# Two expert tiles per store in the dense expert-dot stage of a two-block transformer kernel

## The chip, the cores and the metric

The kernel runs as one program on one core of a Trainium2 chip. The metric is the device time of the whole program in microseconds (us); lower is better. TensorE is called PE here, ScalarE ACT, VectorE DVE, GpSimd POOL and SyncE SP.

## The reference, cut to what matters

512 tokens of 1024 features go through two blocks. The first block ends in a PEER layer: each token chooses 8 x 16 of 16,384 experts, takes the dot of its vector with each chosen expert's row of `peer_u`, applies GELU, weighs it, and sums the chosen rows of `peer_v`.

```python
def chunk_fn(args):
    hx, ix, gx = args
    u = peer_u[ix]
    a = jax.nn.gelu(jnp.einsum('td,thkd->thk', hx, u), approximate=False)
    vsel = peer_v[ix]
    return jnp.einsum('thk,thkd->td', gx * a, vsel)
```

The second block (a convolution, attention and pooling mixer, then 16 experts with 2048 hidden features that each choose their tokens) follows it.

## The kernel before

Of the PEER layer, 128 tokens are computed sparsely (rows gathered by indirect DMAs from POOL) and the other 384 (`DENSE`) densely. The dense part has two stages that concern us.

**First stage** (`peer_first_phase`, class `ExpertDots`). The 16,384 experts are 128 tiles of 128. For a tile, SP loads 512 KB of `u_tiles` (`load`, L548); ACT writes the rounded high part of it (`split_scalar`, a cast recorded at L82); POOL writes the low part (`split_pool`, recorded at L87); PE makes 24 matmuls of 128x384 into one of two PSUM banks (`dot`, L566); ACT applies GELU from the bank into one of two halves of the SBUF buffer `gelu` (`activate`, L574) and then issues, on its own DMA queue, a store of 192 KB to the DRAM tensor `expert_dots` (L577). There are three slots for the loaded tile, one of which lies in `one_h_row` and `one_acts`. Two semaphores `stored[0]` and `stored[1]` tell when the store of each half has landed, and GELU of tile t waits for the store of tile t-2. PE's dots of tile t wait for GELU of tile t-2, which frees the bank.

The order on ACT is written out by hand: split of tile t+2, GELU and store of tile t, and so on. The first 54 tiles run in a loop of 6. From tile 56 on, other work is interleaved: 48 sets of 8 tokens, three for every four tiles, for which DVE builds one-hot matrices, ACT scales them (`gate_set`, L1278), PE makes 16 small matmuls (L1260), and ACT copies the product out (`stage_set`, L1287). After GELU of tile t, ACT does `stage_set` of the set that stood behind tile t-1 on PE and `gate_set` of the one that will stand behind tile t+1. No set stands behind a tile whose number leaves 3 when divided by 4. In this half SP also stores the weights that come of it (`expert_weights`, L1201), POOL gathers `peer_u` rows for the sparse tokens, and DVE reduces them (L1400).

At the end SP loads the first `peer_v` rows and stored dots of the second stage, stores the last weights (3 MB), waits for these, loads the first weights (L2270), and waits for the stores of the dots (L1221). The next stage begins after all engines have ended the first.

**Second stage** (`peer_value_phase`, class `ValueRows`): 64 turns of two expert tiles. Per turn SP reads 384 KB of stored dots (`load_dots`, L2266), 1 MB of `peer_v` (L2262), and for every second turn 768 KB of weights (L2270). DVE multiplies dots and weights to coefficients (L649), ACT and DVE split them and the rows, and PE makes 36 matmuls of 128x512 (L687). Beside it POOL gathers 1 MB of `peer_v` rows per turn for the sparse tokens, which DVE adds (L638).

Of the kernel before, what the change touches and what calls it, by code (L numbers as in the profile page):

```python
# [6 lines left out]
F32 = mybir.dt.float32  # L7
# [6 lines left out]
P = 128  # L14
# [16 lines left out]
ETILES = NKEY  # L31
DENSE = T - P
# [10 lines left out]
class Steps:  # L43


    def __init__(self, eng, sem, base=0):
        self.eng, self.sem, self.base, self.n = eng, sem, base, 0
# [42 lines left out]
def rows(vector_dram, n):  # L90

    return vector_dram.partition_broadcast(n)
# [420 lines left out]
class ExpertDots:  # L513
# [6 lines left out]
    def __init__(self, nc, s, A, h_t, h_row, dots_dram):  # L520
        self.nc, self.A, self.h_t, self.dots_dram = nc, A, h_t, dots_dram
        n = self.SLOTS
        raw = s.sb("u_raw", [P, n - 1, KD, P])
        split = s.sb("u_split", [P, n - 1, 2, KD, P], F32R)
        self.raw = [raw[:, i] for i in range(n - 1)] + [h_row[:].rearrange("p (k e) -> p k e", k=KD)]
        self.split = [split[:, i] for i in range(n - 1)] + [h_t[:, :, :, 0:P]]
        self.gelu = s.sb("gelu", [P, self.OUT, DENSE])
        self.banks = s.ps("dot_ps", [P, self.OUT, BANK])
        self.loaded = [s.sem(f"u_loaded{i}") for i in range(n)]
        self.stored = [s.sem(f"dots_stored{i}") for i in range(self.OUT)]  # L530
        self.hi_ready, self.lo_ready, self.dotted, self.gelu_ready = (s.sem(x) for x in (
            "u_hi_ready", "u_lo_ready", "dotted", "gelu_ready"))

    def credits(self, eng, name):

        if name == "scalar":
            eng.sem_inc(self.gelu_ready, self.OUT)
            for sem in self.stored:
                eng.sem_inc(sem, 16)
        if name == "gpsimd":  # L540
            eng.sem_inc(self.lo_ready, self.SLOTS)
        if name == "tensor":
            eng.sem_inc(self.dotted, self.SLOTS)
# [26 lines left out]

    def activate(self, act, tile, loop, q):
        act.wait_ge(self.dotted, tile + 1 + self.SLOTS)
        act.wait_ge(self.stored[q % 2], loop * 48 + 16 * (q // 2) + 16)
        self.nc.scalar.activation(self.gelu[:, q % 2], self.banks[:, q % 2, 0:DENSE],  # L574
                                  ACT.Gelu).then_inc(self.gelu_ready, 1)
        act.wait_ge(self.gelu_ready, tile + 1 + self.OUT)
        act.dma_start(self.dots_dram[bass.ds(tile, 1)].rearrange("a e t -> e (a t)"),  # L577
                      self.gelu[:, q % 2]).then_inc(self.stored[q % 2], 16)


def peer_value_phase(nc, A, dots_dram, weight_dram, x, gate, expert, slot_coef, gathered, values):
# [547 lines left out]
def peer_first_phase(nc, A, ident, dots, shared, score, choice, h_row, expert, slot_coef, weight_dram, gathered, values):  # L1129
# [10 lines left out]
    with Scope(nc, "peer") as s:  # L1140
# [46 lines left out]
        with nc.Block() as block:  # L1187
            @block.sync
            def _(sp):
                sp.dma_start(iota[:], rows(A["iota"], P)).then_inc(iota_loaded, 16)  # L1190
                sp.wait_ge(h_ready, 1)
                with sp.Fori(0, LOOPS) as i:
                    for j in range(LOOP):
                        dots.load(sp, i * LOOP + j, i, j)
                for j in range(FIRST - LOOPS * LOOP):
                    dots.load(sp, LOOPS * LOOP + j, LOOPS, j)

                def store_part(span, part):
                    if part == 0:
                        sp.wait_ge(staged, PER_SPAN * (span + 1))  # L1200
                    sp.dma_start(weight_dram[span, :, part * PART:(part + 1) * PART, :],  # L1201
                                 stage[:, span % 2, part * PART:(part + 1) * PART, :]).then_inc(stored[span % 2], 16)

                part = 0
                for r in range(LEFT):
                    dots.load(sp, FIRST + r, (FIRST + r) // LOOP, (FIRST + r) % LOOP)
                    while part < PARTS * SPANS and r >= after_tile[PER_SPAN * (part // PARTS + 1) - 1] + 4 + part % PARTS:
                        store_part(part // PARTS, part % PARTS)
                        part += 1
                sp.wait_ge(stored[0], 16 * PARTS * (SPANS // 2))  # L1210
                for turn in range(2):
                    values.load_rows(sp, turn)
                    values.load_dots(sp, turn, dots.dots_dram)
                while part < PARTS * SPANS:
                    store_part(part // PARTS, part % PARTS)
                    part += 1
                for b in range(2):
                    sp.wait_ge(stored[b], 16 * PARTS * (SPANS // 2))
                values.load_weights(sp, 0, weight_dram)
                for b in range(2):  # L1220
                    sp.wait_ge(dots.stored[b], 16 + 16 * ETILES // 2)  # L1221

            @block.gpsimd
            def _(pool):
# [1015 lines left out]
class ValueRows:  # L2240
# [22 lines left out]
            "(a e) d -> e a d", e=P)).then_inc(self.v_loaded[turn % 2], 16)  # L2263

    def load_dots(self, sp, turn, dots_dram):
        sp.dma_start(self.dot[:, turn % 2], dots_dram[2 * turn:2 * turn + 2].rearrange(  # L2266
            "a e t -> e a t")).then_inc(self.dot_loaded[turn % 2], 16)

    def load_weights(self, sp, pair, weight_dram):
        sp.dma_start(self.weight[:, pair % 2].rearrange("p s a t -> p s (a t)"),  # L2270
# [4 lines left out]
def program(nc, A, out, taps=None):  # L2275
# [12 lines left out]
    h_dram = nc.dram_tensor("h_rows", (T, D), F32, kind="Internal").ap()  # L2288
    ada_dram = nc.dram_tensor("ada_rows", (3, 4, BANK), F32, kind="Internal").ap()
    spec_dram = nc.dram_tensor("filter_spectrum", (P, NT, 2, HY), F32, kind="Internal").ap()  # L2290
    dots_dram = nc.dram_tensor("expert_dots", (ETILES, P, DENSE), F32, kind="Internal").ap()
    weight_dram = nc.dram_tensor("expert_weights", (SPANS, NKEY, NKEY, SPAN), F32, kind="Internal").ap()

    with Scope(nc, "all") as g:
# [5 lines left out]
        with Scope(nc, "one") as b1:  # L2300
# [31 lines left out]
            with Scope(nc, "pe") as p:  # L2332
# [7 lines left out]
                with Scope(nc, "dots") as d:  # L2340
                    dots = ExpertDots(nc, d, A, acts, h_row, dots_dram)
# [135 lines left out]
```

## Time and profile before

| what | value |
|---|---|
| median of 3 runs | 3066.65 us (3065.62 to 3068.15) |
| the profiled execution's own time | 3073.93 us |
| its span, first to last instruction | 3072.1 us |
| mean granted TensorE clock in it | 0.945 of full speed |
| first stage, first to last GELU | 521.7 to 1156.1 us of the span |
| second stage's matmuls | from 1174.4 us of the span |
| stores of dots | 128 of 192 KB |
| reads of dots | 64 of 384 KB, 8.6 us median from issue to landing |
| busy PE, DVE, ACT, POOL | 85%, 46%, 27%, 22% of the span |

Times inside the execution are counted from the start of its span. A line such as L574 is a line of the kernel; L82 and L87 are helpers that several stages call, so there the name of the tile tells which work it is. In a timeline a merged row can hold several instructions (x24). What stands in brackets is the idle time before the instruction and what ended it.

### The profile page before, as it was taken

The numbers are of one execution on the slowest core, as the hardware profiler recorded it, in microseconds if no ns is written. First come the engines' busy times: TensorE is split into PE (matmuls) and PEld (weight loads), VectorE is DVE, ScalarE is ACT, GpSimd is POOL, SyncE is SP. The second block draws the span as 40 slices with busy tenths as digits, with TensorE's granted clock in tenths as the row PEclk, the third lists the DMA queues.
The fourth block names the chain that finished last, engine by engine and source line by source line (L and its number), as shares of the span: only waits on it lengthen the run. The fifth ranks groups of instructions, "written<-read, shape, count | busy, mean of one in ns | idle before, by whom it ended". The sixth has DMA issues, their size and how long they took to land. (4 is left out here: it accounts for less than half of the span.)

```text
span 3072.1 us, 33638 instructions
## 1 busy us (share of the span) xinstructions
PE 2620.4 (85%) x12721; PEld 1841.3 (60%) x12721; DVE 1411.2 (46%) x2349; ACT 833.9 (27%) x1375; POOL 667.3 (22%) x421
## 2 busy tenths in 40 slices
PE   5984697999999997999999589775988788788886
PEld 2852577999999996888888467462322223223222
DVE  4326534998877866888878524532000010000001
ACT  1223222334666662333333322421000000000001
POOL 0030002676888872222222001000000000000000
PEclk8996898999999998999999799887999999999999
DMA  5443132555999999999998222129999999999996
GB/s 224 125 161 123 37 110 84 172 173 197 308 375 382 363 345 347 354 351 356 351 352 319 96 65 78 44 108 410 421 421 421 421 421 421 422 421 421 421 421 281
DMA packets 246772, 869.74 MB, mean 283 GB/s; under 512 B 28415, under 2 KB 97663, under 8 KB 194040
## 3 DMA queue, kind: packets, MB, share of 16 engines
q1 hardware_dynamic: 190048, 703.45, 59.6%
q0 software_dynamic: 38016, 138.43, 11.8%
q10 hardware_dynamic: 18584, 26.23, 2.3%
q8 instruction: 76, 1.25, 0.2%
q14 instruction: 48, 0.39, 0.0%
HBM read 812.42 MB, written 55.60 MB: 283 GB/s over the span
## 5 line engine op out<-in xcount | busy, mean ns | idle before, releaser
L687 PE MATMUL val_banks<-val_v,val_coef_split 128*128 128x512 f32 x2304 | 524.8, 390 | 18.3 <-DVE val_coef_split L87 18.3
L687 PEld LDWEIGHTS val_banks<-val_v,val_coef_split 128*128 128x128 f32 x2304 | 434.0, 188 | 109.0 <-DVE val_v L87 18.6
L932 PE MATMUL moe_up_ps<-all_raw_first,all_h_rows 128*64 128x512 f32 x1696 | 422.5, 608 | 74.3 <-DMA all_raw_first<-in_w_up 54.1
L566 PE MATMUL dots_dot_ps<-one_acts,dots_u_split 128*128 128x384 f32 x2064 | 374.5, 338 | 18.0 <-POOL dots_u_split L87 18.0
L566 PEld LDWEIGHTS dots_dot_ps<-one_acts,dots_u_split 128*128 128x128 f32 x2064 | 359.3, 189 | 20.7 <-POOL dots_u_split L87 10.7
L932 PEld LDWEIGHTS moe_up_ps<-all_raw_first,all_h_rows 128*64 128x64 f32 x1696 | 138.3, 139 | 325.7 <-issue 324.5
L87 POOL TENSOR_TENSOR dots_u_split<-dots_u_raw,dots_u_split 128x1024 fp32r<-128x1024 f32 x86 | 227.0, 2641 | 344.0 <-ACT dots_u_split L82 342.9
L1051 DVE TENSOR_TENSOR all_x<-moe_y_ps,all_x 128x512 f32<-128x512 f32 x64 | 44.1, 691 | 558.6 <-PE moe_y_ps L898 558.5
L949 PE MATMUL moe_y_ps<-all_raw_first,moe_hid_t 128*64 128x512 f32 x848 | 203.7, 597 | 42.8 <-DMA all_raw_first<-in_w_down 24.3
L82 ACT CAST val_v<-pe_shared 128x2048 fp32r<-128x2048 f32 x64 | 122.4, 1912 | 355.1 <-PE val_banks L687 336.2
L1121 POOL DMA_INDIRECT val_v_rows<-in_peer_v,one_expert x128 | 123.6, 966 | 410.1 <-DVE val_banks L638 388.3
L87 DVE TENSOR_TENSOR val_v<-pe_shared,val_v 128x2048 fp32r<-128x2048 f32 x64 | 146.7, 2293 | 90.1 <-ACT val_v L82 90.1
L566 PE MATMUL dots_dot_ps<-one_acts 128*128 128x384 f32 x1008 | 183.3, 336 | 3.3 <-POOL one_acts L87 3.3
L1400 DVE CUSTOM_DVE_ANT_0 peer_u_rows<-peer_u_rows,peer_h_ps 128x1024 f32<-128x1024 f32 x128 | 153.6, 1216 | 64.9 <-DMA peer_u_rows<-in_peer_u,one_expert 61.6
L566 PEld LDWEIGHTS dots_dot_ps<-one_acts 128*128 128x128 f32 x1008 | 174.3, 188 | 4.3 <-POOL one_acts L87 4.2
L1057 DVE TENSOR_TENSOR moe_silu<-moe_silu,moe_up_ps 128x512 f32<-128x512 f32 x32 | 22.0, 688 | 328.7 <-PE moe_up_ps L932 328.5
L854 POOL DMA_INDIRECT all_h_rows<-h_rows,moe_token_u x8 | 7.6, 944 | 742.0 <-PE moe_turn_ps L887 496.3
L638 DVE SCALAR_TENSOR_TENSOR val_banks<-val_v_rows,one_slot_coef,val_banks 128x1024 f32<-128x1024 f32 x128 | 164.6, 1286 | 7.1 <-DVE val_banks L638 0.5
L1121 POOL DMA_INDIRECT peer_u_rows<-in_peer_u,one_expert x128 | 153.4, 1198 | 64.8 <-DVE peer_slot_dot L1400 42.7
L949 PEld LDWEIGHTS moe_y_ps<-all_raw_first,moe_hid_t 128*64 128x64 f32 x848 | 67.5, 136 | 157.5 <-issue 156.0
L1380 DVE TENSOR_TENSOR peer_hot<-peer_iota,peer_choice_t 128x1024 f32<-128x1024 f32 x96 | 149.7, 1600 | 12.8 <-issue 9.1
L932 PE MATMUL moe_up_ps<-moe_raw_more,all_h_rows 128*64 128x512 f32 x352 | 109.0, 597 | 15.7 <-DMA moe_raw_more<-in_w_up 7.9
(356 smaller groups left out, 3356.2 us busy)
## 6 DMA issues: line engine op xcount, KB each, us to landing
all_raw_first<-in_w_gate SPq DMA_DIRECT2D x106, 1024.0 KB, 27.3
all_raw_first<-in_w_up SPq DMA_DIRECT2D x106, 1024.0 KB, 27.6
all_raw_first<-in_w_down SPq DMA_DIRECT2D x106, 1024.0 KB, 27.3
pe_shared<-in_peer_v SPq DMA_DIRECT2D x64, 1024.0 KB, 6.9
dots_u_raw<-in_u_tiles SPq DMA_DIRECT2D x86, 512.0 KB
expert_dots<-dots_gelu ACTq DMA_DIRECT2D x128, 192.0 KB
expert_weights<-pe_shared SPq DMA_DIRECT2D x48, 512.0 KB
pe_shared<-expert_dots SPq DMA_DIRECT2D x64, 384.0 KB, 8.6
```

What stands on the lines that cost most here:

```text
L82: return eng.copy(part, src)
L87: return eng.tensor_tensor(part_lo, src, part_hi.bitcast(F32), ALU.subtract)
L566: last = self.nc.tensor.matmul(self.banks[:, q % 2, 0:DENSE], self.split[q % 3][:, u_part, k], self.h_t[:, h_part, k, T - DENSE:T], start= ...
L638: nc.vector.scalar_tensor_tensor(out=sparse_sum, in0=sparse.rows[:, c % sparse.NR, :], scalar=slot_coef[:, c:c + 1], in1=sparse_sum, op0=A ...
L687: last = nc.tensor.matmul(banks[:, 2 * (t + 1) + half, :], coef_split[:, b, c_part, a, t * P:(t + 1) * P], v[:, b, v_part, a, half * BANK: ...
L932: last = nc.tensor.matmul(up_ps[of(e), b, :], xs_t(i)[:, k, of(e)], w[e][:, b * BANK:(b + 1) * BANK], start=(k == 0), stop=(k == KD - 1))
L949: last = nc.tensor.matmul(y_ps[of(e), half, :], hid_t[:, j, of(e)], w[e][:, k * D + half * BANK:k * D + (half + 1) * BANK], start=(j == 0) ...
L1051: nc.vector.tensor_tensor(part, y_ps[:, o % 2, :], part, ALU.add).then_inc(added, 1)
L1057: nc.vector.tensor_tensor(silu[:, b, :], silu[:, b, :], up_ps[:, b, :], ALU.mult).then_inc(hid_ready, 1)
L1121: self.nc.gpsimd.indirect_dma_start(out=self.rows[:, b, :], out_offset=None, in_=self.rows_dram, in_offset=bass.IndirectOffsetOnAxis(ap=se ...
L1380: return nc.vector.tensor_tensor(out[:, n % 2], iota[:].unsqueeze(1).to_broadcast([P, SET, NKEY]), choice_t[:, i, n * SET:(n + 1) * SET].u ...
L1400: nc.vector.tensor_tensor_reduce(out=sparse.rows[:, c % sparse.NR, :], in0=sparse.rows[:, c % sparse.NR, :], in1=h_ps[:].rearrange("p a n ...
```

## The change

The two halves of `gelu` are stored together. GELU of an even tile waits for the store of the pair before (that is, tiles t-2 and t-1), GELU of an odd tile for no store, and only after the odd tile is a store issued: 384 KB, for each of 128 partitions one run of 3072 bytes. The tensor in DRAM is laid out as 64 pairs of `[128, 2, 384]`, so that the second stage's read of a pair is also one run of 3072 bytes per partition, where it was two of 1536. One semaphore takes the place of two. The bytes stored and read stay the same.

```diff
-        self.stored = [s.sem(f"dots_stored{i}") for i in range(self.OUT)]
+        self.stored = s.sem("dots_stored")
...
-            for sem in self.stored:
-                eng.sem_inc(sem, 16)
+            eng.sem_inc(self.stored, 16)
...
         act.wait_ge(self.dotted, tile + 1 + self.SLOTS)
-        act.wait_ge(self.stored[q % 2], loop * 48 + 16 * (q // 2) + 16)
+        if q % 2 == 0:
+            act.wait_ge(self.stored, loop * 48 + 16 * (q // 2) + 16)
         self.nc.scalar.activation(self.gelu[:, q % 2], self.banks[:, q % 2, 0:DENSE],
                                   ACT.Gelu).then_inc(self.gelu_ready, 1)
-        act.wait_ge(self.gelu_ready, tile + 1 + self.OUT)
-        act.dma_start(self.dots_dram[bass.ds(tile, 1)].rearrange("a e t -> e (a t)"),
-                      self.gelu[:, q % 2]).then_inc(self.stored[q % 2], 16)
+        if q % 2 == 1:
+            act.wait_ge(self.gelu_ready, tile + 1 + self.OUT)
+            act.dma_start(self.dots_dram[bass.ds(loop * 3 + q // 2, 1)].rearrange("b e a t -> e (b a t)"),
+                          self.gelu[:].rearrange("p a t -> p (a t)")).then_inc(self.stored, 16)
...
-                for b in range(2):
-                    sp.wait_ge(dots.stored[b], 16 + 16 * ETILES // 2)
+                sp.wait_ge(dots.stored, 16 + 16 * ETILES // 2)
...
-        sp.dma_start(self.dot[:, turn % 2], dots_dram[2 * turn:2 * turn + 2].rearrange(
-            "a e t -> e a t")).then_inc(self.dot_loaded[turn % 2], 16)
+        sp.dma_start(self.dot[:, turn % 2], dots_dram[turn]).then_inc(self.dot_loaded[turn % 2], 16)
...
-    dots_dram = nc.dram_tensor("expert_dots", (ETILES, P, DENSE), F32, kind="Internal").ap()
+    dots_dram = nc.dram_tensor("expert_dots", (ETILES // 2, P, 2, DENSE), F32, kind="Internal").ap()
```

## Rows read from the trace of the kernel before

**Rows 1.** Busy time of each engine by stretch; then clock, DMA share, GB/s.

```profile
748.00:1157.00 409.00, 394.04 (x2519) 387.76 (x2517) 301.25 (x358) 268.90 (x580) 327.18 (x197) 1.00 0.94 350
1157.00:1174.00 17.00, 0.00 (x0) 0.00 (x0) 5.06 (x6) 4.83 (x4) 4.43 (x3) 0.55 0.72 253
522.00:748.00 226.00, 226.00 (x1306) 226.00 (x1305) 219.99 (x731) 84.44 (x110) 155.97 (x57) 1.00 0.53 172
1175.00:1696.00 521.00, 521.00 (x2291) 431.15 (x2290) 419.28 (x383) 164.77 (x125) 118.50 (x125) 1.00 0.96 345
```

**Rows 2.** What PE waited for, 760 to 1160 us: total, times, longest.

```profile
PE dots_dot_ps L566 <- POOL dots_u_split L87: 8.2, 8, 1.7
...
PE dots_dot_ps L566 <- POOL one_acts L87: 2.4, 2, 1.6
```

**Rows 3.** The same for ACT, 760 to 1160 us.

```profile
ACT dots_gelu L574 <- PE dots_dot_ps L566: 82.1, 48, 4.1
...
ACT dots_u_split L82 <- DMA dots_u_raw<-in_u_tiles: 15.7, 12, 3.6
ACT one_acts L82 <- DMA one_h_row<-in_u_tiles: 7.3, 5, 2.6
```

**Rows 4.** Timeline of ACT at 605 us, in the loop.

```profile
604.88 0.49 ACT L574 ACTIVATE dots_gelu<-dots_dot_ps 128x384 f32<-128x384 f32 x1 [2.05 <-PE dots_dot_ps L566]
605.54 0.34 ACTq L577 DMA_DIRECT2D expert_dots<-dots_gelu  x1
...
608.96 0.49 ACT L574 ACTIVATE dots_gelu<-dots_dot_ps 128x384 f32<-128x384 f32 x1 [1.92 <-PE dots_dot_ps L566]
```

**Rows 5.** Timeline of ACT and PE at 886 us, tiles 79 to 81.

```profile
885.99 0.49 ACT L574 ACTIVATE dots_gelu<-dots_dot_ps 128x384 f32<-128x384 f32 x1 [2.37 <-PE dots_dot_ps L566]
886.51 0.34 ACTq L577 DMA_DIRECT2D expert_dots<-dots_gelu  x1
...
887.80 2.45 ACT L1278 ACTIVATE peer_hot<-peer_hot,peer_choice_t 128x128 f32<-128x128 f32 x8
...
890.35 2.02 PE L1260 MATMUL peer_banks<-peer_hot 128*128 128x128 f32 x16 [0.24 <-issue]
...
891.09 0.48 ACT L574 ACTIVATE dots_gelu<-dots_dot_ps 128x384 f32<-128x384 f32 x1
...
891.99 2.46 ACT L1278 ACTIVATE peer_hot<-peer_hot,peer_choice_t 128x128 f32<-128x128 f32 x8 [0.41 <-ACT dots_gelu L574]
...
896.38 1.95 PE L1260 MATMUL peer_banks<-peer_hot 128*128 128x128 f32 x16
```

**Rows 6.** DMA issues of the whole execution: KB each, median us to landing.

```profile
expert_dots<-dots_gelu ACTq DMA_DIRECT2D x128, 192.0 KB
...
pe_shared<-expert_dots SPq DMA_DIRECT2D x64, 384.0 KB, 8.6
...
val_v_rows<-in_peer_v,one_expert POOLq DMA_INDIRECT x128, 7.1
h_rows<-all_h_rows SPq DMA_DIRECT2D x4, 512.0 KB, 8.8
out<-all_x SPq DMA_DIRECT2D x4, 512.0 KB, 2.6
```

**Rows 7.** DMA queues, 850 to 1140 us: packets, MB, share of 16 engines.

```profile
q1 hardware_dynamic: 12632, 45.96, 41.3%
q10 hardware_dynamic: 7344, 10.03, 9.3%
```

**Rows 8.** Timeline at the end of the first stage, tiles 125 to 127.

```profile
1148.83 0.34 ACTq L577 DMA_DIRECT2D expert_dots<-dots_gelu  x1
...
1151.92 0.49 ACT L574 ACTIVATE dots_gelu<-dots_dot_ps 128x384 f32<-128x384 f32 x1 [3.12 <-PE dots_dot_ps L566]
...
1156.61 0.34 ACTq L577 DMA_DIRECT2D expert_dots<-dots_gelu  x1
...
1165.68 0.37 SPq L2270 DMA_DIRECT2D pe_shared<-expert_weights  x1
```

## The prediction

> **What bounds the kernel now.** I read the profile in this order: busy time by stretch around the changed code, then what PE and ACT waited for there, then the timeline of single tiles, then the DMA issues and queues. The stretches divide the changed code into four parts [rows 1]. In the loop (522 to 748 us) PE is busy for 226.00 of 226 us: PE is the bound, and DMA stands at a share of 0.53. From 748 to 1157 us PE runs for 394.04 of 409 us and DMA has a share of 0.94: still PE, with 15 us in which it does not run. From 1157 to 1174 us PE rests for 17 us while DMA drains. In the second stage PE is busy for 521.00 of 521 us, though DMA's share is 0.96 there. So what the change can give back is at most the 15 us and part of the 17 us. What it can cost is any wait that reaches PE.
>
> PE's waits in the second part are for POOL's low parts, 8.2 and 2.4 us [rows 2]. Behind them stand loads that land late: ACT waits 15.7 and 7.3 us for them [rows 3]. No GELU waits for a store there or anywhere in the first stage; nearly all of GELU's idle time is ended by PE (82.1 us in this part) [rows 3].
>
> **The new wait.** Before, the store of tile t-2 had almost two tile times to land. Now the pair's store is issued behind the odd tile and must land before the next even GELU, one tile time later. What does that gap hold?
>
> In the loop: issue at 605.54, next GELU at 608.96 [rows 4], a gap of 3.4 us. If the store takes longer, GELU slips, but two things take up the slip. A tile time is 608.96 - 604.88 = 4.1 us [rows 4], and the bank that GELU frees is wanted only one tile time after its dots end. Of that 4.1 us GELU itself takes 0.49, and it starts some 0.2 us after the matmuls, so 3.4 us of slip cost PE nothing. The split queued behind it on ACT is for three tiles on, and it has about as much room with its 1.05 us and POOL's 2.4 us. The landing can take 3.4 + 3.4 = 6.8 us before PE waits.
>
> In the second part the tight case is an even tile behind one whose number leaves 3 by 4, since PE has no set between them. Tile 79's store is issued at 886.51, tile 80's GELU starts at 891.09: a gap of 4.6 us, already filled by ACT's own work (stage, gate, split) [rows 5]. Queued behind tile 80's GELU is the gate of the set that follows tile 81, which PE takes up at 896.38 [rows 5]. The gate takes 2.46 us, and GELU with its hand-over 0.5 us, so GELU may start as late as 896.2 - 2.5 - 0.5 = 893.2. A landing of 893.2 - 886.5 = 6.7 us from issue is the point at which PE begins to wait. The change helps here a little: an even tile has no store to issue, so the 0.4 us between GELU and gate [rows 5] goes. There are some 16 such tight tiles. The other even tiles have PE's 1.95 us set [rows 5] within their gap and no gate behind GELU, so they bear about 2 us more.
>
> **How long the store takes.** The trace has no landing for the dots' stores, since nobody waited for them [rows 6]. From below: 512 KB to DRAM on quiet queues land in 2.6 us [rows 6]; 384 KB cannot do much better, say 2.3. From above: 512 KB stores issued four together have a median of 8.8 us, and 384 KB reads in a queue behind others 8.6 us [rows 6]. The nearest case under load is the gather of 512 KB in the second stage, 7.1 us [rows 6], where DMA is as busy as here. I read it as some 1.3 us of fixed time (half of what the 2.6 us store took) and 5.8 us of transfer; three quarters of the transfer is 4.3 us, so 5.6 us in all. ACT's queue holds nothing else, and its store is alone in it, so I take 5 us in the second part (near the gather, somewhat under it) and 3 to 4 in the loop at half the DMA share. Both are under 6.7 us: tight GELUs slip 5.0 - 4.6 = 0.4 us and PE loses nothing. Both ends are kept: 2.6 us costs 0; 8.8 us costs (8.8 - 6.7) x 16 = 34 us.
>
> In the Trainium skill, "DMA: Bandwidth & Descriptors", the section on where the fixed cost goes says that the completion is held until the last byte is confirmed and that writes to HBM can be surprisingly slow in this, about 2 us in all. No run here shows that split; with 2 us fixed the estimate would be about 6 us, still under the point where PE waits.
>
> **The other edits.** 64 store issues of 0.34 us go from ACT. PE waits for POOL and not for ACT's issue, so I count 0; the direct bound is the 15 us of rows 1. Bytes: the ACT queue moved 10.03 MB at 9.3% of 16 engines for 290 us, 431 us of engine time or 23.2 bytes per ns; the SP queue, with mostly larger packets, 45.96 MB at 41.3%, or 24.0 [rows 7]. Runs twice as long can thus save about 3% of a 9.3% share: 0.3% of 290 us, under 1 us of DMA time. In the second stage the same applies to 384 KB of some 2.8 MB per turn, while PE leaves no gap: 0. The loop's address arithmetic is a few register instructions: 0.
>
> **End of the first stage.** Tile 125's store is issued at 1148.83; tile 126's GELU at 1151.92 [rows 8] would slip to 1153.8, which no one misses, since tile 127's GELU must wait for PE until about 1156.1 anyway. The last store, now 384 KB, goes out at 1156.61 and lands at 1161.6, before the weights let SP go on at 1165.68 [rows 8]. Cover 4 us, cost 0. With 8.8 us for both stores it would land at 1167.5, so 1.8 us later.
>
> **Sum.** Loop 0, second part 0 with up to 1 us of disturbed order between splits, gathers and loads, junction 0, second stage 0: +1 us on the profiled 3073.93 us. That execution is 7.3 us (0.24%) above the median of the runs, and I carry the difference over to the median: 3066.65 + 1 = 3067.5 us.
>
> **Rivals.**
> *Slower: the lost double buffer reaches PE.* The landing in the second part passes 6.7 us on the tight tiles. For it: DMA share 0.94 with three queues at work, and landings of 7.1 to 8.8 us are common in this trace. Against it: an otherwise empty queue. At 7.7 us it costs 16 x 1.0 = 16 us, giving 3083 us; at 8.8 us, 34 + 2 us, giving 3103. It decides at 6.7 + 6/16 = 7.1 us, where 6 us are lost.
> *Faster: longer runs and fewer issues relieve the crowded part.* Loads land sooner, ACT's 23 us of waits for them [rows 3] and PE's 10.6 us for POOL [rows 2] shrink. If all 15 us that PE does not run went, 3052 us; half of it, 3059. Against it: under 1 us of DMA time is saved, and bytes are the same. The Trainium skill speaks for this rival on the page "DMA: Bandwidth & Descriptors", section on bandwidth: it wants DMAs batched to 1 MiB or more, and shows larger ones nearer the peak. By that rule both the stores and the crowded stage gain; the queue rows above, 23.2 against 24.0 bytes per ns, agree in direction but leave little of it.
> *No effect in the second stage* is part of the forecast; if it were DMA that set the turns there, the read's part of DMA time, an eighth of it, would shrink by 3%: 0.4% of 521 us, 2 us. It decides nothing.
>
> **How the numbers follow.** 0.2% or 6 us is about what a measurement of this kernel can tell from no change. The forecast has 0.73, and its own range is 3061 to 3072.5; the slower rival 0.15, the faster 0.12. Up to 3059 lies a third of the faster rival, above 3078 about half of the slower one; the range 3059 to 3078 leaves out a little over 0.1. Faster 0.12, same 0.73, slower 0.15.
>
> **What would show it.** In the changed profile the stores stand as 64 of 384 KB, with a landing time now that someone waits: near 5 us. ACT's waits get a new row, GELU waiting for this store, with short waits (under 1 us each in the tight tiles). PE's rows for the four stretches stay at 226 of 226, about 394 of 409 and 521 of 521. The packets fall by 8192 for the stores and 8192 for the reads. I am wrong if the landing passes 7 us, if PE's waits for POOL or for gates grow beyond the 10.6 us, or if the second part becomes shorter than some 403 us.

## The result, and the profile after

The changed kernel takes 3075.41 us (median of 20 runs, 3069.59 to 3084.45), the kernel before, in as many runs, 3069.69 us (3064.93 to 3076.2). The ratio is 1.0018, with a 95% interval of 1.0012 to 1.0025: slower by some 5.5 us, which is real and just under the 0.2% that the prediction counts as no change.

By stretch (busy time of PE, PEld, DVE, ACT, POOL; clock, DMA share, GB/s) the changed kernel shows:

```profile
522.00:748.00 226.00, 225.21 (x1300) 224.90 (x1299) 216.43 (x711) 81.02 (x110) 152.19 (x59) 1.00 0.55 178
748.00:1157.00 409.00, 393.34 (x2495) 384.98 (x2494) 304.70 (x358) 262.23 (x575) 322.22 (x195) 1.00 0.92 344
1177.00:1698.00 521.00, 521.00 (x2289) 431.14 (x2290) 419.30 (x384) 164.73 (x125) 118.69 (x125) 1.00 0.95 345
```

The loop and the second stage stand as they did [rows 1]. The middle part looks almost the same here too, because fixed borders hide a shift: this execution came to tile 54 earlier and to the second stage later. The changed code is better measured from event to event, from the GELU of tile 54 (the end of the loop) to the first matmul of the second stage. Before, that was 746.24 to 1174.38, 428.1 us; now it is 742.74 to 1176.89, 434.2 us. These 6 us are the loss (one profiled execution of each kernel; the table below shows how far such stretches scatter). From there to the end both kernels take 1898 us.

What ACT waited for from 760 to 1160 us in the changed kernel (total, times, longest):

```profile
ACT dots_gelu L574 <- DMA expert_dots<-dots_gelu: 65.7, 28, 6.5
ACT dots_gelu L574 <- PE dots_dot_ps L565: 50.8, 25, 5.2
...
ACT dots_u_split L82 <- DMA dots_u_raw<-in_u_tiles: 9.9, 3, 5.1
...
ACT one_acts L82 <- DMA one_h_row<-in_u_tiles: 2.0, 1, 2.0
```

and what PE waited for in the same time:

```profile
PE peer_banks L1260 <- issue: 12.3, 19, 3.0
PE dots_dot_ps L565 <- POOL one_acts L87: 1.6, 1, 1.6
PE dots_dot_ps L565 <- POOL dots_u_split L87: 1.4, 2, 1.1
```

GELU now waits for the store, 28 times and for 65.7 us. Of this little reaches PE: its waits ahead of the small matmuls of the sets, 2.5 us before, are 12.3 us. Its waits for POOL fell from 10.6 us [rows 2] to 3.0 us, and ACT's for late loads from 23 us [rows 3] to 11.9: it looks as if the loads catch up while PE stands at a set, so that part of the new wait takes the place of an old one. (In the run with the gate ahead, below, where PE does not stand there, its waits for POOL are back at 9.2 us.)

One tight tile shows the way. This is the timeline of ACT and PE at 909 us, tiles 83 to 85:

```profile
909.38 0.34 ACTq L578 DMA_DIRECT2D expert_dots<-dots_gelu  x1
...
914.99 4.42 PE L565 MATMUL dots_dot_ps<-one_acts,dots_u_split 128*128 128x384 f32 x24
917.61 0.49 ACT L574 ACTIVATE dots_gelu<-dots_dot_ps 128x384 f32<-128x384 f32 x1 [3.56 <-DMA expert_dots<-dots_gelu]
918.00 2.44 ACT L1278 ACTIVATE peer_hot<-peer_hot,peer_choice_t 128x128 f32<-128x128 f32 x8
...
920.53 2.02 PE L1260 MATMUL peer_banks<-peer_hot 128*128 128x128 f32 x16 [1.12 <-issue]
```

The store goes out at 909.38 and GELU of tile 84, which waits for its landing, starts at 917.61, 8.2 us later. It has waited 3.56 us, the gate of the next set starts behind it at 918.00 and ends at 920.44, and PE, done with the dots of tile 85, has stood for 1.12 us before the 16 matmuls that need this gate. In the kernel before, the tight tile 80 had a landing that nobody waited for and a gate that was ready 1.9 us early [rows 5].

Where a GELU is released by the store, its start less the store's issue is taken as the landing. In the loop the profile names 13 of them, 4.3 to 5.1 us (median 4.5); from tile 56 to 123 it names 28, 5.2 to 8.5 us (median 7.1). The profile's attribution leaves out the longest, at tile 72 (timeline of ACT and PE):

```profile
835.71 4.32 PE L565 MATMUL dots_dot_ps<-one_acts,dots_u_split 128*128 128x384 f32 x24
836.43 0.34 ACTq L578 DMA_DIRECT2D expert_dots<-dots_gelu  x1
...
842.05 4.41 PE L565 MATMUL dots_dot_ps<-one_acts,dots_u_split 128*128 128x384 f32 x24
846.52 0.49 ACT L574 ACTIVATE dots_gelu<-dots_dot_ps 128x384 f32<-128x384 f32 x1 [5.25 <-PE dots_dot_ps L565]
...
849.44 2.66 PE L1260 MATMUL peer_banks<-peer_hot 128*128 128x128 f32 x16 [2.98 <-issue]
```

The idle time is put down to PE, because the dots of tile 73 happened to end at 846.46. But the dots that this GELU needs are those of tile 72, and they ended at 840.03. What was missing was the store, whose last packet ended at 845.9. The landing was 10.1 us, and the PE wait of 2.98 us behind it is the longest of all.

There are 15 tight tiles from 64 to 120 (numbers divisible by 4). Tile by tile, the start of GELU less the issue of the store has a median of 7.5 us, and PE waits at the next set in just the nine of them where it is over 7.1 us:

| tile | 72 | 76 | 84 | 88 | 96 | 104 | 108 | 116 | 120 |
|---|---|---|---|---|---|---|---|---|---|
| landing, us | 10.09 | 7.54 | 8.23 | 7.26 | 7.71 | 8.48 | 7.65 | 7.77 | 7.99 |
| PE waits, us | 2.98 | 0.41 | 1.12 | 0.14 | 0.43 | 1.28 | 0.53 | 0.65 | 0.85 |

The difference is 7.1 to 7.3 us each time. That is the point of the prediction, 6.7 us, and the 0.4 us that it named and did not add: an even tile has no store to issue between GELU and gate. In sum the nine wait 8.4 us. The row above leaves out the shortest and counts the other eight, 8.3 of its 12.3 us; 1.7 us stand behind a load that landed late (0.8 us at the same place before), and the rest are waits of at most 0.24 us, which the kernel before has too.

The packets of ACT's queue (q10) give the landing of every store, waited for or not: 128 runs and 16 packets of 4 bytes each. GELU starts 0.4 to 0.8 us after the last of them has ended. From issue to that end the 34 pair stores of the tiles 55 to 121 take 2.0 to 9.5 us, median 5.9, so the medians above, of those that were waited for, lean high. About half of it, 3.0 us in the median, passes before the store's first packet starts: from 909.38 to 912.9 the two other queues fill the engines and q10 moves nothing. In the loop the 27 pair stores take 2.0 to 4.7 us, median 2.9, with the first packet after 0.8.

At the end of the stage (timeline of ACT):

```profile
1151.89 0.35 ACTq L578 DMA_DIRECT2D expert_dots<-dots_gelu  x1
1158.36 0.49 ACT L574 ACTIVATE dots_gelu<-dots_dot_ps 128x384 f32<-128x384 f32 x1 [6.50 <-DMA expert_dots<-dots_gelu]
1159.02 0.49 ACT L574 ACTIVATE dots_gelu<-dots_dot_ps 128x384 f32<-128x384 f32 x1 [0.16 <-PE dots_dot_ps L565]
1159.54 0.34 ACTq L578 DMA_DIRECT2D expert_dots<-dots_gelu  x1
```

The longest wait of all, 6.50 us, costs nothing: the last GELU still starts as soon as PE has ended. The packets fell by 17,409, from 246,772: 8192 for the reads on q1 (190,048 before) and 9216 on q10 (18,584 before). The last number is 1024 more than was predicted, the 4-byte packets of 64 stores. The lines for all DMA and for the two queues read:

```profile
DMA packets 229363, 869.73 MB, mean 283 GB/s; under 512 B 27391, under 2 KB 63871, under 8 KB 176632
...
q1 hardware_dynamic: 181856, 703.45, 59.4%
...
q10 hardware_dynamic: 9368, 26.23, 2.2%
```

### The profile page after: what moved, and what is told of

Read it like the earlier page. It is cut to its first block and busy times, and to the rows that moved or that the text cites. A ratio compares the mean times of both kernels' runs of the same rounds, so it can differ in the third digit from the quotient of the medians.

```text
span 3074.4 us, 33453 instructions
## 1 busy us (share of the span) xinstructions
PE 2624.3 (85%) x12721; PEld 1841.4 (60%) x12721; DVE 1413.8 (46%) x2349; ACT 825.6 (27%) x1375; POOL 660.8 (21%) x421
## 3 DMA queue, kind: packets, MB, share of 16 engines
q0 software_dynamic: 38016, 138.43, 11.9%
## 5 line engine op out<-in xcount | busy, mean ns | idle before, releaser
L688 PE MATMUL val_banks<-val_v,val_coef_split 128*128 128x512 f32 x2304 | 524.8, 390 | 17.9 <-DVE val_coef_split L87 17.9
L688 PEld LDWEIGHTS val_banks<-val_v,val_coef_split 128*128 128x128 f32 x2304 | 434.0, 188 | 108.6 <-DVE val_v L87 18.2
L1380 DVE TENSOR_TENSOR peer_hot<-peer_iota,peer_choice_t 128x1024 f32<-128x1024 f32 x96 | 154.0, 1644 | 26.5 <-PE peer_banks L1260 19.5
L574 ACT ACTIVATE dots_gelu<-dots_dot_ps 128x384 f32<-128x384 f32 x128 | 62.8, 491 | 255.0 <-PE dots_dot_ps L565 147.6
```

Source lines behind the costliest of these rows:

```text
L688: last = nc.tensor.matmul(banks[:, 2 * (t + 1) + half, :], coef_split[:, b, c_part, a, t * P:(t + 1) * P], v[:, b, v_part, a, half * BANK: ...
L1380: return nc.vector.tensor_tensor(out[:, n % 2], iota[:].unsqueeze(1).to_broadcast([P, SET, NKEY]), choice_t[:, i, n * SET:(n + 1) * SET].u ...
```

## The experiments

The first two rows are the 20 runs each of the section above. The others come from two groups of five interleaved rounds, 11 executions of each kernel (4 of the short runs), and their ratios are against the kernel before in the same rounds (3069.12 us in the first group, 3069.41 in the second). "Stretch" is the time from the GELU of tile 54 to the second stage's first matmul in the profiled execution.

| kernel | median us | ratio (95%) | stretch us |
|---|---|---|---|
| before | 3069.69 | 1 | 428.1 |
| changed | 3075.41 | 1.0018 (1.0012 to 1.0025) | 434.2 |
| read only | 3069.10 | 0.9995 (0.9986 to 1.0004) | 427.3 |
| wait only | 3073.42 | 1.0015 (1.0005 to 1.0025) | 434.0 |
| three pair buffers | 3068.49 | 0.9995 (0.9986 to 1.0004) | 429.0 |
| gate first | 3070.95 | 1.0002 (0.9993 to 1.0011) | 426.4 |
| short runs | 3098.72 | 1.0098 (1.0082 to 1.0113) | 452.7 |
| three buffers, short runs | 3068.09 | 0.9994 (0.9985 to 1.0003) | 428.2 |
| gate first, on before | 3069.95 | 1.0002 (0.9993 to 1.0011) | 428.9 |
| three buffers, gate first | 3067.99 | 0.9995 (0.9986 to 1.0004) | 429.9 |

The stretch sorts the kernels into 426 to 430 us without the loss (seven kernels), 434 with it (two), and 453.

**The new layout and read alone** (from the kernel before).

```diff
-        act.dma_start(self.dots_dram[bass.ds(tile, 1)].rearrange("a e t -> e (a t)"),
+        act.dma_start(self.dots_dram[bass.ds(loop * 3 + q // 2, 1), :, q % 2].rearrange("b e t -> e (b t)"),
                       self.gelu[:, q % 2]).then_inc(self.stored[q % 2], 16)
...
-        sp.dma_start(self.dot[:, turn % 2], dots_dram[2 * turn:2 * turn + 2].rearrange(
-            "a e t -> e a t")).then_inc(self.dot_loaded[turn % 2], 16)
+        sp.dma_start(self.dot[:, turn % 2], dots_dram[turn]).then_inc(self.dot_loaded[turn % 2], 16)
```

> The stored pairs lie in DRAM as in the changed kernel, so the second stage reads runs of 3072 bytes, but each tile is stored by itself (192 KB, runs of 1536 bytes) into its half of the run, and GELU of tile t waits for the store of tile t-2 as before. The theory (the whole loss is the wait of an even GELU for the pair's store) expects the time of the kernel before, ratio 1.000 within 0.001, and no wait of ACT for a store. The rival that the layout itself matters (half runs side by side in DRAM, or the longer reads) expects some of the loss of 0.18% or a gain to be seen here: at least 3 us away from before, and a second stage whose 521 us change.

The time is that of before, and ACT has no row of waiting for a store. The read's longer runs bring nothing that can be measured, and the new layout costs nothing measurable either.

**The wait alone.** To the kernel above only this was added:

```diff
-        act.wait_ge(self.stored[q % 2], loop * 48 + 16 * (q // 2) + 16)
+        if q % 2 == 0:
+            for b in range(2):
+                act.wait_ge(self.stored[b], loop * 48 + 16 * (q // 2) + 16)
```

> The kernel that differed from before by nothing that was seen (pairs side by side in DRAM, one store of 192 KB per tile with runs of 1536 bytes), with the wait alone of the changed kernel: an even GELU waits for the stores of both tiles of the pair before. The odd tile's store is 8 packets per engine, as many as the pair's store of the changed kernel, half as long each. The theory of turns per packet expects landings barely shorter than in the changed kernel (8 packets less some 60 ns each, 0.5 us), so medians near 6.5 us in the crowded part, PE's waits for gates of 6 to 12 us there, and ratio 1.0005 to 1.002. If the landing went with the bytes, it would be near half: under 4.6 us in nearly all tiles, no slip and ratio 1.000 or less.

The loss is back, 1.0015, though every store is 192 KB. What ACT and PE waited for, 760 to 1160 us:

```profile
ACT dots_gelu L576 <- DMA expert_dots<-dots_gelu: 55.6, 23, 6.1
...
PE peer_banks L1262 <- issue: 12.2, 21, 3.1
```

The waits of PE are those of the changed kernel (12.3). By start of GELU less issue, landings of half the bytes are hardly shorter where DMA is crowded: 5.2 to 9.7 us, median 7.1, in the 23 tiles of 56 to 123 that waited; in the 15 tight ones 7.1 against 7.5. It was expected near 6.5.

Two things have to be kept in mind in this comparison. In 24 of the 34 cases the store of the even tile was still under way in the same queue when that of the odd tile was issued, so the half-sized store was not alone. By the packets (issue to the last one's end) the median over all 34 is 5.5 us against 5.9; over the ten without such an overlap it is 5.1, against 5.3 for the same tiles of the changed kernel. So the bytes count for little there. All the kernels together say the same: medians of 5.5 to 6.3 us in the four with 192 KB stores, 5.5 to 6.2 in the four with 384 KB in 128 runs. And PE begins to wait at a landing of 6.6 us here, not 7.1, since an even tile has a store to issue behind its GELU again. The shorter landing and the earlier point nearly cancel, which is why PE's waits are the same.

**Three pair buffers** (from the changed kernel).

```diff
-        self.gelu = s.sb("gelu", [P, self.OUT, DENSE])
+        self.gelu = s.sb("gelu", [P, 3, 2, DENSE])
...
-        self.stored = s.sem("dots_stored")
+        self.stored = [s.sem(f"dots_stored{i}") for i in range(3)]
...
-            act.wait_ge(self.stored, loop * 48 + 16 * (q // 2) + 16)
+            act.wait_ge(self.stored[q // 2], loop * 16 + 16)
```

> The changed kernel with room for three pairs of activated tiles instead of one, and a semaphore for each: an even GELU waits for the pair store three pairs back. Stores stay at 384 KB with runs of 3072 bytes. The theory (the wait is the loss) expects no wait of GELU for a store, PE's waits for gates back from 12.3 to some 2.5 us, and the time of the kernel before or up to 2 us better, ratio 0.999 to 1.0005. The rival (bursts of 384 KB disturb loads and gathers in the crowded part) expects the loss to stay: ratio 1.0015 or more, with last dots at about 1159 us.

No GELU waits for a store any more, and the loss is gone, with the 384 KB stores and their bursts as they were. PE waits at sets for 1.2 us, and its waits for POOL are back, as are ACT's for loads:

```profile
PE dots_dot_ps L566 <- POOL dots_u_split L87: 8.7, 10, 1.4
PE dots_dot_ps L566 <- POOL one_acts L87: 3.3, 4, 1.6
PE peer_banks L1262 <- issue: 1.2, 5, 0.2
```

So bursts are not the cause. Nor do they help: 0.9995 can't be told from 1. The stores still land nearly as late (issue to last packet, median 5.5 us over the same 34 tiles); only nobody waits.

**The gate ahead of GELU.** From the changed kernel, in the part after the loop:

```diff
+                    gate_first = r % 2 == 0 and set_of(r + 1) is not None
+                    if gate_first:
+                        gate_set(set_of(r + 1))
                     dots.activate(act, FIRST + r, (FIRST + r) // LOOP, (FIRST + r) % LOOP)
...
-                    if set_of(r + 1) is not None:
+                    if set_of(r + 1) is not None and not gate_first:
                         gate_set(set_of(r + 1))
```

> The changed kernel with one order on ACT changed: in the second part, gate_set of the set behind tile r+1 stands ahead of GELU of an even tile r, where it stood behind it. The theory (the slipped GELU costs PE time only through the gate queued behind it) expects GELU to wait for the store as long as before or a little less, but PE's waits for gates to fall from 12.3 to under 4 us, and the time to be that of the kernel before, ratio 0.999 to 1.001. The rival (the slip reaches PE by the bank or by the split and POOL) expects PE's waits to stay at 15 us or more in sum and a ratio of 1.0015 or more.

The landings are as long as before this edit (5.7 to 8.8 us, median 7.6, from tile 56 to 123), and GELU still waits 40.2 us for them, but PE's waits at sets are 2.0 us and the time is back (1.0002). Tile 84 again, timeline of ACT and PE:

```profile
910.99 2.45 ACT L1278 ACTIVATE peer_hot<-peer_hot,peer_choice_t 128x128 f32<-128x128 f32 x8
...
914.32 0.49 ACT L574 ACTIVATE dots_gelu<-dots_dot_ps 128x384 f32<-128x384 f32 x1 [0.88 <-DMA expert_dots<-dots_gelu]
...
917.85 1.95 PE L1260 MATMUL peer_banks<-peer_hot 128*128 128x128 f32 x16
```

The landing takes 7.9 us here, past the 7.1, and PE starts the set with no idle time. The gate was done at 913.44. The slip reached PE through what stood behind GELU on ACT, not through the bank or the split.

**The same order on the kernel before**, as a control.

> A control: the kernel before with the gate of the following set ahead of GELU of an even tile, as in the run that mended the changed kernel. If that run gained by the slip alone, this one shows the time of before, ratio 0.9990 to 1.0005. The rival is that the new order is better by itself (earlier gates for PE), which would show as 3 us or more here too, ratio 0.999 or less, and would mean that the mended run owes part of its gain to something else than the slip.

1.0002: the order brings nothing measurable of its own. What it mended in the changed kernel was the slip.

**Pair stores in runs of 1536 bytes** (from the changed kernel, with the old layout and read).

```diff
-            act.dma_start(self.dots_dram[bass.ds(loop * 3 + q // 2, 1)].rearrange("b e a t -> e (b a t)"),
-                          self.gelu[:].rearrange("p a t -> p (a t)")).then_inc(self.stored, 16)
+            act.dma_start(self.dots_dram[bass.ds(loop * 6 + q - 1, 2)].rearrange("a e t -> e a t"),
+                          self.gelu[:]).then_inc(self.stored, 16)
```

> The changed kernel with one store per pair and the wait of the even GELU, but the DRAM tensor laid out per tile as before, so that the store is 256 runs of 1536 bytes, and so is the read. If the DMA engines share their time between queues packet by packet, the store now has 16 packets per engine to get through instead of 8, each behind one packet of each other queue: landings in the crowded part grow from 5.2 to 8.5 us to 7 to 12 us, every tight tile passes the 6.7 us, and the kernel loses 30 to 60 us (ratio 1.01 to 1.02). If queues share by bytes, or if the landing is fixed time, the landings stay as they are and so does the time, ratio 1.001 to 1.003.

A loss of 30 us, 1.0098, from four executions of 3090.43 to 3107.15 us, of which the profiled one is the fastest (its stretch is 24.6 us longer than before). The bytes are the same and the packets of each store twice as many. Nine of the 24 landings seen from tile 56 on are over 8.5 us, up to 12.4 us, where the changed kernel had one; the median, 7.2, did not move. So it was not "every tight tile" as expected: landings start at 5.0 us, and seven of the 15 tight tiles pass 6.7. In the loop the median is 4.6 (4.5 before the edit). The worst tile, 72, in the timeline:

```profile
840.53 4.44 PE L565 MATMUL dots_dot_ps<-one_acts,dots_u_split 128*128 128x384 f32 x24
...
847.27 0.49 ACT L574 ACTIVATE dots_gelu<-dots_dot_ps 128x384 f32<-128x384 f32 x1 [7.65 <-DMA expert_dots<-dots_gelu]
847.66 2.43 ACT L1278 ACTIVATE peer_hot<-peer_hot,peer_choice_t 128x128 f32<-128x128 f32 x8
...
850.19 3.38 PE L1260 MATMUL peer_banks<-peer_hot 128*128 128x128 f32 x16 [5.23 <-issue]
```

The same chain as at tile 84 above, with 5.23 us of idle PE instead of 1.12. Six tight tiles pass 7.1 us, by 20.2 us in sum, and PE waits 19.5 us behind them. Two even tiles that are not tight, 86 and 94, have landings of 9.7 and 10.2 us and cost 1.3 and 1.6 us, so their point is near 8.5 us. In all, PE waits 27.2 us at sets:

```profile
PE peer_banks L1260 <- issue: 27.2, 20, 5.2
```

**Three buffers with short runs.**

> Pair stores of 256 runs of 1536 bytes, and reads of the same kind, as in the run with short runs that lost 1%, but with three pair buffers, so that no GELU should wait. The theory (the 1% was the wait for a landing of up to 12 us, not the load on the DMA engines) expects the time of the kernel before, ratio 0.999 to 1.001, and no row of GELU waiting for a store. The rival (256 packets in one burst hold up loads and gathers) expects a good part of the 1% to stay: ratio 1.003 or more.

0.9994. With the wait taken away, the 256 short packets of a store cost nothing that can be measured. So the 1% of the run above was waiting for landings, and not a load on the DMA engines that reached PE by way of loads or gathers.

This run and the first one with three buffers also give the fairest comparison of the two run lengths, since nobody waits in either. From issue to last packet the 34 stores have a median of 5.5 us with 128 runs and 7.5 us with 256; 27 of the 34 are longer, and the longest grows from 7.8 to 11.0 us. In the loop both medians are 4.0. (Where GELU waits, in the run above, the median with 256 runs is 5.8 us. These are single profiled executions.)

**Both remedies together.**

> Both remedies on the changed kernel: three pair buffers and the gate ahead of the even GELU. The theory expects nothing beyond either one, since each takes away the same loss: ratio 0.998 to 1.0005. If the two losses are separate they add up, to 3 us or more better than before, ratio 0.999 or less.

0.9995, as either alone. None of these versions beats the kernel before by anything measurable; against the changed kernel the three buffers win back the loss.

## Why the prediction was right, and where it was off

The time (3067.5 forecast, by its own sum 3067.65; 3075.4 measured) lies in the range, and the change of 0.18% within the 0.2% that was called the same. But it is above the 3072.5 us up to which the forecast gave its own range, and 3 us of the distance are only that the kernel before measures 3069.69 in 20 runs and not 3066.65. Against the kernel before in the same runs it is +5.5 us where +1 was forecast. Two of the prediction's own signs of being wrong came true: landings pass 7 us, and PE's waits for POOL and for gates together grew from 13.1 to 15.3 us, those for gates alone to 12.3, beyond the 10.6. So the number was right and the mechanism behind it ("PE loses nothing") was not. The slower rival's mechanism, which had a chance of 0.15, is what happened, at a small sum. That part was luck.

- *Loop: 0.* Right. GELU slips there by about 1 us in 13 tiles. A landing of 3 to 4 us was taken; by the packets it is 2.9 in the median, some 3.4 with the hand-over to GELU, and 5.1 at most, under the 6.8 us that GELU was said to bear (no run reaches that point). PE is busy for 225.2 of 226 us.
- *The point at which PE begins to wait, 6.7 us.* Right in its working, 0.4 us low: 7.1 us, as the nine tiles above show, with the issue that goes. In the wait-only run, which keeps that issue, it is 6.6. For the other even tiles "about 2 us more" was said; 8.5 us was seen.
- *The landing in the crowded part, 5 us.* This is the mis-sized term: 5.9 us to the last packet in the median of all 34, so about 6.4 us at GELU, and 7.5 in the tight tiles, up to 10.1. The nearest row, the gather's 7.1 us, had been scaled down by bytes to 5.6 and then lowered again for an otherwise empty queue. The empty queue did not help: 3.0 us pass before the first packet. More than the median it was the spread that was missing from the sum: one value stood for all tiles, and even a true median of 6.4 would have said "no cost", while nine tiles of 15 were past the point.
- *"The trace has no landing for the dots' stores."* It has, in the packets of q10. In the kernel before, the 34 stores of odd tiles from 55 to 121 took 1.6 to 8.4 us to the last packet, median 6.1. Tile 79, on which the prediction worked out its gap, is one of the quick ones with 3.0. Tile 71, issued at 840.03, is the slow one; counted in windows from its issue to 846.8 and to 848.5:

```profile
q10 hardware_dynamic: 90, 0.14, 5.4%
...
q10 hardware_dynamic: 144, 0.20, 6.2%
```

- *Cost of the slips, 0 to 34 us.* 8.4 us of PE's waits are due to landings, and its waits at sets grew by 9.8 us in all, less 7.6 us of waits for POOL that went. That leaves 2.2 of the 6 us of the stretch. PE's time not busy in it grew by 2.0 us (from 32.3 of 428.1 to 34.4 of 434.2); the other 4.0 us stand as busy time, where the ends of matmuls are modelled, and can't be placed by these records. What the runs show is that the stretch is back at 426 to 430 us once the wait is gone or the gate stands ahead of it.
- *Junction: 0.* Right for the reason given: the last stores are covered by the stores of weights. The second stage starts 17.9 us after the last dots, 18.3 before.
- *Second stage, read: 0.* Right; 521 of 521 us, and the read-only run is at 0.9995.
- *ACT's 64 issues fewer: 0.* Right, as the three-buffer run shows, which has the same 64 fewer and gains nothing measurable.
- *The faster rival.* Excluded, by the two runs in which the wait is gone and the long runs and large stores remain. The rule of the Trainium skill that it leaned on, in "DMA: Bandwidth & Descriptors", section on bandwidth (batch DMAs towards 1 MiB), did not decide the time here: PE set the pace. It would have cost a buffer wait to follow it with two halves.

The Trainium skill's section on queues, rings and completion order, on the same page, says that each DMA engine goes round its queues packet by packet. The runs are in line with it so far: in the crowded part half the bytes in as many packets took about as long, and as many bytes in twice the packets took 2 us longer where nobody waited. But a packet of that section holds several descriptors, while a packet of the profile is one run here, and no run varied the other queues' packets, so the sharing itself was not measured.

## What to carry to other kernels

Merging two stores into one over the same two buffers turns double buffering into single buffering: what had two tile times to land now has one. Ask what is queued behind the waiting instruction on its engine, work out the landing time at which the bound engine starts to wait, and compare that with landings under load in the same stretch, without scaling them down by size, and with their spread and not only their median. They can be read before the change is made, even where nobody waits: count the packets on the store's queue in a window that starts at its issue. If the batch is wanted, give it another buffer, or put the work that the bound engine needs ahead of the wait.

## What the runs showed of the hardware that was not expected

- Where three queues are at work (DMA share 0.92), a DRAM store of 384 KB takes 2.0 to 9.5 us from issue to its last packet (median 5.9), and one of 192 KB with as many packets 1.5 to 8.7 (median 5.5, in the wait-only run). In the loop, at a share of 0.55, the 384 KB take 2.0 to 4.7 us, median 2.9. In the crowded part the time goes with the traffic beside it more than with the store's own bytes, and half of it passes before the first packet.
- The length of runs that brought nothing for throughput (three buffers: 0.9995 with 3072 bytes, 0.9994 with 1536) made 30 - 5.5, about 24 us where a landing was waited for. Run length was a matter of latency here: medians of 5.5 against 7.5 us where DMA is crowded and nobody waits, no difference in the loop.
